# A two-layer block on one core: head norms' roots on another engine, attention heads at every second unit, decay rows from two rounded products

## The reference

```python
h = rms_norm(x, g_mix)
q, k, v, z, xbc, dt_raw = split(h @ w_in)            # 16 heads of 64; z 1024, xbc 2048, dt 16 wide
# attention: each head's q and k are normalised and rotated, then a softmax over the causal scores
q = rope(rms_norm(q, g_q)) * 64 ** -0.5              # rms_norm: x * rsqrt(mean(x * x) + EPS) * g
k = rope(rms_norm(k, g_k))
attn = rms_norm(sum_over_patterns(softmax(q @ k.T)) @ v, g_attn_out)
# state space scan: chunks of 128 tokens, 16 heads, 4 groups
a_cs = cumsum(dt * a)                                # per head, within a chunk
l_mat = exp(a_cs[l] - a_cs[s])  for l >= s           # the decay from token s to token l
y = (c @ b.T * l_mat * dt) @ x + (c @ state) * exp(a_cs) + d_skip * x
ssm = rms_norm(y * silu(z), g_ssm_out)               # per group
x = x + concat(attn, ssm) @ w_out
```

## Time and profile before

| | us |
|---|---|
| median of three runs | 3859.56 (3859.32 to 3861.42) |
| the profiled execution's own time | 3862.77 |
| its span in the profile | 3861.0 |
| mean granted TensorE clock | 0.925 |

### The profile page before, as it was taken

How to read it: one execution, slowest core, us unless ns; L and a number is a source line. 1 busy time by engine, 2 the same in 40 slices (tenths; PEclk the granted TensorE clock), 3 DMA queues, 4 the chain that set the end, 5 groups by cost and what they waited for, 6 DMA issues and landing times.

```text
span 3861.0 us, 53072 instructions
## 1 busy us (share of the span) xinstructions
PE 3285.4 (85%) x20976; PEld 2734.2 (71%) x20976; DVE 2473.2 (64%) x3281; ACT 1432.5 (37%) x2059; POOL 850.5 (22%) x623
## 2 busy tenths in 40 slices
PE   8988998999999999999999996766666667666678
PEld 8977888999999999999998996732222223222248
DVE  6567865654455556874546666977777776555566
ACT  6555555553354444564445452220100001100025
POOL 2000011000000100000000021255665565565522
PEclk9998999999999999999999997878878888888899
DMA  6433243556556565455553456899999999999974
GB/s 227 151 99 110 94 158 120 166 183 188 180 183 189 177 207 176 161 181 185 164 179 101 148 185 221 313 355 421 421 422 421 422 421 420 422 421 421 422 288 148
DMA packets 188024, 952.86 MB, mean 247 GB/s; under 512 B 20992, under 2 KB 21120, under 8 KB 121984
## 3 DMA queue, kind: packets, MB, share of 16 engines
q0 software_dynamic: 73728, 536.90, 33.7%
q1 hardware_dynamic: 114048, 412.56, 33.2%
HBM read 947.29 MB, written 2.10 MB: 246 GB/s over the span
## 4 chain that ended last, share of the span: by engine, by line
PE 57%; DMA 19%; DVE 13%; POOL 4%; ACT 4%; issue 3%; DVEq 0%; ACTq 0%; SPq 0%; POOLq 0%
PE ps L529 56%; DMA BIG<-in_peer_v,CS 7%; DMA HLF<-in_peer_v,CS 6%; DMA HF<-in_peer_v,CS 3%; DVE HL L1755 3%; POOL HLF L511 2%; DVE BIG L1759 2%; POOL BIG L511 2%; DVE BIG L2393 1%; DMA BIG<-in_peer_u,CS 1%; DVE BIG L1755 1%; DMA HLF<-in_peer_u,CS 1%; ACT BIG L1117 1%; ACT HL L1123 1%; PE ps L533 1%
## 5 line engine op out<-in xcount | busy, mean ns | idle before, releaser
L529 PE MATMUL ps<-HS,HL 128*128 128x256 f32 x10128 | 1340.8, 288 | 36.8 <-DVE HL L1755 31.3
L529 PEld LDWEIGHTS ps<-HS,HL 128*128 128x128 f32 x10128 | 1288.0, 196 | 48.6 <-DVE HL L1755 36.2
L1755 DVE TENSOR_TENSOR HL<-RAW,HL 128x1024 fp32r<-128x1024 f32 (+1 forms) x772 | 954.1, 1236 | 246.2 <-ACT HL L1123 181.6
L1123 ACT CAST HL<-RAW 128x1024 fp32r<-128x1024 f32 (+1 forms) x772 | 805.3, 1043 | 499.9 <-PE ps L529 431.8
L529 PE MATMUL ps<-BIGR,HL 128*128 128x256 f32 x6720 | 897.5, 286 | 24.0 <-DVE HL L1755 14.4
L529 PEld LDWEIGHTS ps<-BIGR,HL 128*128 128x128 f32 x6720 | 853.9, 194 | 32.3 <-issue 15.5
L529 PE MATMUL ps<-BIG,HF 128*128 128x512 f32 (+1 forms) x744 | 387.7, 671 | 187.5 <-DMA BIG<-in_peer_v,CS 164.1
L529 PE MATMUL ps<-HLF,HF 128*128 128x512 f32 x648 | 341.1, 679 | 162.1 <-DMA HLF<-in_peer_v,CS 148.8
L529 PEld LDWEIGHTS ps<-BIG,HF 128*128 128x128 f32 (+1 forms) x744 | 158.1, 223 | 412.4 <-issue 378.7
L478 POOL COPY NSUM<-TMP 128x256 f32<-128x256 f32 x6 | 3.3, 552 | 1948.7 <-ACT TMP L1119 1948.7
L2393 DVE CUSTOM_DVE_ANT_0 BIG<-BIG 128x2048 f32<-128x2048 f32 x133 | 304.9, 2293 | 164.1 <-DMA BIG<-in_peer_u,CS 155.1
(11 more groups left out here) (196 smaller groups left out, 2239.6 us busy)
## 6 DMA issues: line engine op xcount, KB each, us to landing
RAW<-in_w_up SPq DMA_DIRECT2D x128, 512.0 KB, 3.8
RAW<-in_w_down SPq DMA_DIRECT2D x128, 512.0 KB, 4.2
RAW<-in_w_out SPq DMA_DIRECT2D x64, 512.0 KB, 3.6
RAW<-in_w_qk SPq DMA_DIRECT2D x32, 512.0 KB, 3.3
RAW<-in_w_xbc SPq DMA_DIRECT2D x32, 512.0 KB, 3.4
RAW<-in_w_xr SPq DMA_DIRECT2D x32, 512.0 KB, 3.4
RAW<-in_w_yr SPq DMA_DIRECT2D x32, 512.0 KB, 3.4
RAW<-in_w_gr SPq DMA_DIRECT2D x32, 512.0 KB, 3.8
```

Source lines behind the costliest of these rows:

```text
L529: return e.matmul(o, l, r, start=start, stop=stop, skip_group_check=True)
L1123: s.done(e.copy(o, i), sig)
L1755: v.done(e.tensor_tensor(o, a, b, op), sig)
```

## The change

Three edits. (1) The head norms' roots and reciprocal become one power of -1/2 on GpSimd: VectorE adds the epsilons to SS, GpSimd takes the power, VectorE multiplies by it. (2) In `attn_heads`, on all three engines, a head begins only in every second step. (3) ACS is cut into two parts in the rounded type, a cast by ScalarE and the rest by VectorE, and each row is spread by two rounded products that add up, not by one f32 product; the identity's columns are copied to SEL in that type. The parts lie in CS1's place.

```diff
+        CS1R = sb("CS1R", [128, 2, T], R32)
+        SEL = sb("SEL", [128, 16], R32)
+        ACS_HALVES = [CS1R[0:16, j, :] for j in range(2)]
...
 # GpSimd, between the square sums of g_mix and those of g_cross
+            g.wait_ge(s_con, 16)
+            for G in range(4):
+                g.wait_ge(s_gsum, G + 1)
+                g.done(e.tensor_tensor(SS, SS, con("minus_half").to_broadcast([128, 16]), ALU.pow), (s_grt, G + 1))
...
 # TensorE, ssd_head
-                mm(score_bank(k)[:, 0:T], con("ident")[0:16, h:h + 1].to_broadcast([16, 128]), ACS, True,
-                   True).then_inc(s_score, 1)
+                pe.wait_ge(s_acslo, 1)
+                sel = SEL[0:16, h:h + 1].to_broadcast([16, 128])
+                mm(score_bank(k)[:, 0:T], sel, ACS_HALVES[0], True, False)
+                mm(score_bank(k)[:, 0:T], sel, ACS_HALVES[1], False, True).then_inc(s_score, 1)
...
 # TensorE, ScalarE and VectorE, attn_heads
-                live, h = [], 0
+                live, h, rest = [], 0, 0
                 while h < 16 or live:
-                    if h < 16 and ready[0] > h // 4:
+                    if h < 16 and ready[0] > h // 4 and rest == 0:
                         live.append(attn(h))
-                        h += 1
+                        h, rest = h + 1, 2
+                    rest = max(rest - 1, 0)
...
 # ScalarE, prepared
-                t = SS.rearrange("p (i a) -> p i a", i=2)
                 act(TMP[:, 0, :], TG[G % 2], ACT.Square, (s_gsq, G + 1))
                 yield
-                s.wait_ge(s_gsum, G + 1)
-                act(t[:, :, 0:4], t[:, :, 0:4], ACT.Sqrt, bias=con("eps64"))
-                act(t[:, :, 4:8], t[:, :, 4:8], ACT.Sqrt, (s_grt, G + 1), bias=con("eps"), scale=1.0 / 64)
...
 # ScalarE, ssd_pre, its fifth step
+                s.wait_ge(s_acs, 1)
+                copy(SEL[0:16, :], con("ident")[0:16, 0:16])
+                copy(ACS_HALVES[0], ACS, (s_acshi, 1))
...
 # VectorE, prepared
-                total(SS, TMP[:, 0, :].rearrange("p (a d) -> p a d", d=64), ALU.add, False, (s_gsum, G + 1))
+                total(SS, TMP[:, 0, :].rearrange("p (a d) -> p a d", d=64), ALU.add, False)
+                t = SS.rearrange("p (i a) -> p i a", i=2)
+                ts(t[:, :, 0:4], t[:, :, 0:4], 64 * EPS, None, ALU.add)
+                ts(t[:, :, 4:8], t[:, :, 4:8], 1.0 / 64, EPS, ALU.mult, ALU.add, (s_gsum, G + 1))
                 yield
                 v.wait_ge(s_grt, G + 1)
-                recip(SS, SS)
...
 # VectorE, ssd_pre, its last two steps
                     copy(dst, PS[3][:, 0:32].rearrange("p (i h) -> p i h", i=2), (s_free3, t))
+                    if j:
+                        v.wait_ge(s_acshi, 1)
+                        tt(ACS_HALVES[1], ACS, ACS_HALVES[0].bitcast(F32), ALU.subtract, (s_acslo, 1))
```

More of the change, by code:

```diff
@@ L22 @@
 CONSTS = [("ident", 128), ("ones", 128), ("rot2", 128), ("triu", 128), ("sel1", 7), ("mask", 384),
-          ("iota", 16), ("invf", 8), ("eps", 1), ("eps128", 1), ("eps64", 1)]
+          ("iota", 16), ("invf", 8), ("eps", 1), ("eps128", 1), ("minus_half", 1)]
 VECS = [("g_mix", 16), ("g_cross", 16), ("g_mem", 16), ("g_mlp", 16), ("attn_norm", 16), ("ffn_norm", 16),
@@ L213, in build @@
         VEC = sb("VEC", [128, nvec])
-        CS1 = sb("CS1", [128, 2, T])
+        with nc.sbuf_tensor("CS1", [128, 2, T], F32) as CS1:
+            pass
+        CS1R = sb("CS1R", [128, 2, T], R32)
+        SEL = sb("SEL", [128, 16], R32)
         TMP = sb("TMP", [128, 2, 1024])
@@ L372, in build @@
         s_sin = sem("sin_ready")
-        s_gsq, s_gsum, s_grt, s_qkr = sem("qk_squares"), sem("qk_squares_summed"), sem("qk_roots"), sem("qk_roped")
+        s_gsq, s_gsum, s_grt, s_qkr = sem("qk_squares"), sem("qk_means"), sem("qk_roots"), sem("qk_roped")
         s_turn3, s_free3 = sem("turn3_filled"), sem("turn3_free")
         s_max, s_exp, s_prob = sem("row_max"), sem("row_exp"), sem("probs_ready")
-        s_acs = sem("decay_sums")
+        s_acs, s_acshi, s_acslo = sem("decay_sums"), sem("decay_sums_high"), sem("decay_sums_low")
         s_zs, s_conv, s_silu = sem("z_silu"), sem("conv_done"), sem("xbc_silu")
@@ L2548, in constants @@
     c["eps128"] = np.full((128, 1), 128 * EPS)
-    c["eps64"] = np.full((128, 1), 64 * EPS)
+    c["minus_half"] = np.full((128, 1), -0.5)
     return np.concatenate([np.asarray(c[n], np.float32).reshape(128, k) for n, k in CONSTS], axis=1)
```

## The result

The changed kernel takes 3849.34 us (median of nine runs, 3847.35 to 3854.69); the kernel before took 3862.18 in the runs beside it. The ratio is 0.9972, 95% interval 0.9964 to 0.9980: 10.8 us faster, 0.28%; the two medians lie 12.8 us apart. The forecast was 3836 us, 23.5 us faster. The measured time lies in the stated range (3822 to 3856) and the direction was right, but the gain is about half of the forecast by the medians and less than half by the ratio.

The account below looks back on a forecast made before the run. The prediction took the kernel as close to TensorE's own work, losing time in short holes and lowered clock. Its terms, 16 + 4 + 1 + 2.5 = 23.5 us, took the median 3859.56 us to 3836, range 3822 to 3856.

Parts of the forecast that it names:

- The first group: First head norm, without attention beside it: 25.4 us for eight units, 0.5 idle; no gain or loss entered in the sum.
- any price under 2.5 us is hidden: GpSimd's power in the head norms: VectorE's other work covers it below 2.5 us; 1 to 2 us taken, at no cost.
- the shadow: VectorE's work between a norm's sum and its scaling: a low half (1.23 us) and a head's mask and maxima (1.30).
- rival 2: The power is slow: above 7 us VectorE stands and PE starves after about 6 us more; 3880 at 20 us; chance 0.08.
- The three groups: Three stretches with head norms and four heads each: 16 us gained of a ceiling of 22.1, lower bound 6.
- rival 1: Holes close only in part: bursts in step 16 still starve PE once per group, the clock falls; 3852 us; chance 0.15.
- the burst is 1 us over and not 2, and the low half runs two units ahead: Step 16 with the scaling: VectorE's load falls from 6.1 to 5.2 us, against some 4.2 for TensorE's unit.
- The last group and the softplus: 278.6 to 310 us, VectorE the bound: two heads' 2.0 us each leave the burst; 4 us gained, 1 to 8.
- the scan's start: Scan three steps later: the turns' 4.3 us hole goes, a second state norm hole costs 4; net 1 us, -4 to 5.
- the decay rows: Two rounded products per head for one f32 product: 0.2 to 0.4 us saved each, 16 heads; 2.5 us, 0 to 6.
- half of them lie where VectorE sets the pace: Decay rows in the scan: half the heads' saving of 3.2 to 6.4 us does not count, so 2.5 us.
- the signs named in the prediction: Signs of being right included stretches of 34 to 36 us, power under 2.5 us, PE never idle over 1 us for the copy.

Follow-up runs that it names:

- e7: The changed kernel with the last group's heads (12 to 15) in every step; 3849.68 us, ratio 0.9979.
- e6: The changed kernel with a product in place of the power on GpSimd, so scaling wrongly; 3844.28 us, ratio 0.9963.
- e12: The kernel of e8 with the turns of q and k one step later too; 3838.91 us, ratio 0.9939 to the kernel before.
- e8: The changed kernel with each head norm's scaling and rotation one step later, the turns where they were; 3841.94 us, ratio 0.9964.
- e10: The kernel before with three empty steps between the attention's end and its output norm, so the scan starts later; 3860.06 us, ratio 0.9998.
- e3: The kernel before with only the decay rows by two rounded products; 3859.57 us, ratio 1.0000.
- e11: The kernel before with each decay row's f32 product issued twice, the second over the first; 3861.70 us, ratio 1.0001.
- e4: The changed kernel without the roots on GpSimd: heads at every second step and rounded decay rows kept; 3852.34 us, ratio 0.9985.
- e2: The kernel before with only heads at every second step, roots still on ScalarE; 3854.58 us, ratio 0.9982.
- e1: The kernel before with only the roots moved to GpSimd; 3855.27 us, ratio 0.9986.

## Why the prediction was wrong

By w_out's start the forecast's terms and the profile's are these.

**The first group: 0 forecast, 5.0 lost (3.6 in e7's profile of the same code).** The failed step reads "any price under 2.5 us is hidden", with "I take 1 to 2 us". The price was 2.90 us, and 3.98 the first time, between my two bounds. Worse, I took the shadow, a low half and a head's mask and maxima, from the second group and applied it to all four. The first group has no heads beside it: its shadow is one low half, 1.23 us. Also missing was a root's way in the first group before, which had no exponentials ahead of it and took 1.92 us: no 6.95 us to beat. And rival 2's "PE starves after about 6 us more" was wrong: 2.83 us of standing made a hole of 2.85 us, because the low half stands behind the scaling in VectorE's queue. Shown by e6 and e12, where the loss is gone.

**The three groups: 16 forecast, 12.3 measured (8.1 in e7's profile of the same code), 9.5 with the short product.** The holes did close in part, as in rival 1. The failed step is "the burst is 1 us over and not 2, and the low half runs two units ahead", which counted only what VectorE owes TensorE directly. A late mask holds ScalarE's exponentials, and behind these stands the emptying of a bank: 5.0 us of TensorE's waits, and the clock falls behind them. In e8 these waits are gone and B gains 14.8 us, in e12 18.0 of the 22.1, so the size was within reach. How much of the shortfall is the waits and how much the clock's chance is open, since the same code gave 12.3 and 8.1.

**The last group and the softplus, the scan's start, the decay rows: 4 + 1 + 2.5 forecast, 2.1 measured together.** The scan's start is worth 1.3 to 1.8 us (e10), about as forecast, though the 4.3 us of the turns went into low-half holes. The decay rows' products are shorter by 0.2 us each, as estimated, and worth nothing (e3). The failed step is "half of them lie where VectorE sets the pace": TensorE has room in all of the scan (e11), although it is busy in 47 of 50 us there by this window of the kernel before. A busy share near the whole did not mean that it set the pace.

```profile
390.00:440.00 50.00, 47.02 (x335) 40.37 (x334) 43.39 (x93) 27.68 (x46) 0.00 (x0) 1.00 0.32 103
```

The softplus's term keeps about 0.7 us of 4. By w_xbc 11 the changed kernel has gained 3.1 us, so the burst did shrink; up to w_z 10 it then gains less than e10, which has the same late scan and dense heads (3.9 and 2.8 us against 5.2 and 3.5). I read this as the two heads that leave the burst and come back behind it; e7, with the last group dense, keeps as much over C, D and E (2.2 us). I had not counted where moved work arrives.

**Right:** the table loads and roots on TensorE's path (e4 without that part gains 3.8 us in B, with it 12.3, or 8.1 in e7); the loads gone, seven of eight; the turns' hole gone and a new one beside the second norm, 2.69 us against 3.13; no cost of the casts. The load shown of e2 takes 1.28 us; it begins 0.07 us behind the operation ahead of it, and the next follows 0.02 us behind it. The Trainium skill ("ScalarE: Activation LUTs", section What ACT_TABLE_LOAD costs) adds a drain of 1.38 us to each switch; this trace has no room for one there. Of the signs named in the prediction, three failed narrowly: the stretches with heads are 37.0, 35.2 and 36.9 us, not all 34 to 36; the power is over 2.5 us; and TensorE still waits up to 1.5 us for ScalarE's copy in them.

From w_out's start to the end the profile of the changed kernel gains 2.6 us more. Those of e1, e2 and e3 gain 1.6 to 3.9 us there too, although nothing differs after w_z, and that of e10 gains nothing. No run shows why; it bounds what a single profile can say about the end. The differences of the medians agree with the sums by w_out within 3.5 us in all kernels.

Left open is also what a power at another place would do (in ScalarE's or VectorE's queue); no kernel with one was run.

## What to carry to other kernels

A hand-over to another engine needs its shadow counted in each place where it occurs, with what stands in that very step; the pipeline's first turn has no neighbours to hide behind. Before shortening anything, put the long operation and its reader one more step apart: by the profiles that one empty step brought 7 us here, more than two of the three edits did alone, and its own cost, the waits before the turns, went when the turns moved too (e12). A gain read at a point in the middle must be followed to where the moved work arrives: 9.0 us by w_z 10 were 1.3 by w_out. And where holes let the clock fall, take a second profile of the same code before reading differences of a few us.

## What the hardware showed unexpectedly

GpSimd's power of 128x16 takes 2.90 us, thirteen times the product of the same operands (0.22 us) and three times an addition of 128x256 (0.88 us). The first of the four, after 83 us of idle time, takes 1.04 to 1.08 us more, for the product (1.26 us) as for the power (3.98 us). The idle time alone does not explain it: in the changed kernel a copy of 128x256 takes 0.40 us after 17 us of idle time and 0.40 us after 255 us. It is also the first instruction of that line of the program; no run separates the two.

The clock made small holes large, and by different amounts: 2.85 us of standing in the first group cost 5.0 us in all, with the stretch's mean clock at 0.89. In e7 and e1 the same hole cost 3.6 and 3.7 us, with 0.94; e12 has no such hole and 1.00. In the changed kernel the granted clock is 1.00 (2.4 GHz) ahead of the hole and 0.50 (1.2 GHz) through the 24 matmuls behind it, which take 5.49 us; the next 24 have 1.00 and take 3.12. The Trainium skill ("TensorE: Matmul & The Clock Gate", section What's actually happening) gives 1.2 GHz after idleness and 2.4 GHz after sustained activity as the two levels, and the rows agree.
